# Softmax probabilities scaled ahead of their transposes, one head on VectorE and one on GpSimd

## The reference, cut to what matters

```python
def one(qblk):
    s = jnp.einsum('bqhd,bkhd->bhqk', qblk, k).astype(jnp.float32) * scale
    p = jax.nn.softmax(s, axis=-1).astype(v.dtype)
    return jnp.einsum('bhqk,bkhd->bqhd', p, v)
```

## Time and profile before

| what | value |
|---|---|
| median of 3 runs | 1138.98 us (1138.32 to 1143.58) |
| span of the profiled execution | 1138.1 us |
| TensorE busy (matmul) | 1042.1 us, 92% |
| VectorE busy | 337.7 us, 30% |
| ScalarE busy | 256.1 us, 23% |
| GpSimd busy | 113.0 us, 10% |
| DMA | 313.84 MB, mean 276 GB/s |

### The profile page before, as it was taken

One profiled execution on the slowest core, in us unless ns is written; L12 is line 12 of the kernel. 1 busy time (PEld: TensorE's weight loads), 2 busy tenths in 40 slices (PEclk: granted clock), 3 DMA queues, 4 the chain that ended last, 5 costly groups with the idle time before them and its releaser, 6 DMA issues. The chain is left out here.

```text
span 1138.1 us, 16374 instructions
## 1 busy us (share of the span) xinstructions
PE 1042.1 (92%) x6617; PEld 506.9 (45%) x6617; DVE 337.7 (30%) x838; ACT 256.1 (23%) x604; POOL 113.0 (10%) x137
## 2 busy tenths in 40 slices
PE   5899899998999999988699989999989999998967
PEld 3445456654434444333244554666444344433324
DVE  3100465412722222112330026542173222221224
ACT  2110254512211111111221014542131111111132
POOL 4120100001001111110022020000010111111000
PEclk8899999998999999999899999999989999999997
DMA  9941466614899999999994225662298999999981
GB/s 351 384 159 74 158 233 222 222 40 162 322 332 322 401 393 397 398 402 411 385 340 154 84 103 223 223 222 75 100 349 305 353 344 395 401 396 412 410 317 56
DMA packets 70291, 313.84 MB, mean 276 GB/s; under 512 B 7786, under 2 KB 10054, under 8 KB 49984
## 3 DMA queue, kind: packets, MB, share of 16 engines
q1 hardware_dynamic: 61280, 288.54, 66.3%
q0 software_dynamic: 8064, 21.01, 5.3%
q10 hardware_dynamic: 864, 3.15, 0.7%
HBM read 301.32 MB, written 18.58 MB: 281 GB/s over the span
## 5 line engine op out<-in xcount | busy, mean ns | idle before, releaser
L938 PE MATMUL psum<-arena 128*64 128x512 f32 x512 | 236.1, 608 | 18.1 <-DMA arena<-in_w_up 11.6
L941 PE MATMUL psum<-arena 128*64 128x512 f32 x512 | 236.6, 609 | 0.0
L938 PEld LDWEIGHTS psum<-arena 128*64 128x64 f32 x512 | 69.1, 140 | 164.9 <-issue 162.6
L992 PE MATMUL psum<-arena 128*64 128x512 f32 x512 | 120.5, 602 | 3.8 <-ACT arena L1399 2.1
L1775 DVE SCALAR_TENSOR_TENSOR arena<-arena,psum 64x768 f32<-64x768 f32 (+1 forms) x32 | 26.1, 814 | 273.0 <-ACT arena L1393 273.0
L1258 PE MATMUL psum<-arena 128*128 128x384 f32 x256 | 86.3, 492 | 0.0
L1393 ACT ACTIVATE arena<-psum 64x768 f32<-64x768 f32 (+1 forms) x32 | 22.3, 697 | 280.3 <-PE psum L941 280.3
L1113 PE MATMUL psum<-arena 128*128 128x384 f32 x256 | 83.5, 487 | 1.2 <-PE psum L1101 0.6
L941 PEld LDWEIGHTS psum<-arena 128*64 128x64 f32 x512 | 69.1, 140 | 0.0
L1113 PEld LDWEIGHTS psum<-arena 128*128 128x128 f32 x256 | 48.3, 190 | 36.9 <-issue 4.0
L1258 PEld LDWEIGHTS psum<-arena 128*128 128x128 f32 x256 | 47.5, 190 | 32.4 <-issue 0.7
(11 more groups left out here) (273 smaller groups left out, 1245.9 us busy)
## 6 DMA issues: line engine op xcount, KB each, us to landing
arena<-in_w_down SPq DMA_DIRECT2D x64, 1024.0 KB, 16.7
arena<-in_w_gate SPq DMA_DIRECT2D x54, 1024.0 KB, 14.5
arena<-in_w_up SPq DMA_DIRECT2D x54, 1024.0 KB, 17.0
arena<-in_w_ada SPq DMA_DIRECT2D x24, 2048.0 KB, 7.9
arena<-in_w_in SPq DMA_DIRECT2D x6, 2048.0 KB, 17.2
arena<-in_w_gate SPq DMA_DIRECT2D x20, 512.0 KB, 17.5
arena<-in_w_up SPq DMA_DIRECT2D x20, 512.0 KB, 18.5
arena<-in_w_out SPq DMA_DIRECT2D x4, 2048.0 KB, 7.9
```

The lines of the kernel that those rows point to most:

```text
L938: ins = nc.tensor.matmul(bank[b][0:MAIN, :], hg[:, k, 0:MAIN], row(wg[half], k), start=(k == 0), stop=(k == KD - 1))
L941: ins = nc.tensor.matmul(bank[b][MAIN:P, :], hg[:, k, 0:MAIN], row(wu[half], k), start=(k == 0), stop=(k == KD - 1))
L992: ins = nc.tensor.matmul(bank[6][MAIN * j:MAIN * j + MAIN, :], hidT[:, c, 0:MAIN], w[half][:, c % 2, 512 * j:512 * j + 512], start=(c == 0 ...
```

## The change

The scaling by the reciprocal sums moves from the attention output to the probabilities. After `rsum` is written, VectorE multiplies head 1's probabilities in place, and GpSimd those of head 0, in place too. TensorE waits for the product of each head before it transposes it, in place of waiting for the exponentials. The two small matmuls that spread the reciprocals go, ScalarE's copy of bank 4 is 128 columns shorter, and `outputs` becomes a copy. `reciprocals(u)` also waits until GpSimd is done with unit u-2, since it overwrites the same places of `rsum`.

```diff
+        prob_pool, prob_dve = sem("prob_pool"), sem("prob_dve")
...
         @block.gpsimd
...
                 pool.sem_inc(out_free, 1)
 
+                for u in range(UNITS):
+                    n = unit(u)[3]
+                    pool.wait_ge(rsum_ready, UNITS * l + u + 1)
+                    pool.tensor_scalar(prob[:, u % 2, 0, 0:n], prob[:, u % 2, 0, 0:n], rsum[:, 2 * (u % 2):2 * (u % 2) + 1], None,
+                                       ALU.mult).then_inc(prob_pool, 1)
...
                 def turned(u):
                     n = unit(u)[3]
-                    pe.wait_ge(exp_ready, UNITS * l + u + 1)
                     for i in (1, 0):
+                        pe.wait_ge(prob_pool if i == 0 else prob_dve, UNITS * l + u + 1)
                         if u >= 1:
                             pe.wait_ge(probT_act if i == 0 else probT_dve, UNITS * l + u)
                         for c in range(n // P):
                             ins = nc.tensor.transpose(bank[4 + i][:, P * c:P * c + P], prob[:, u % 2, i, P * c:P * c + P], ident)
-                        if i == 0:
-                            pe.wait_ge(rsum_ready, UNITS * l + u + 1)
-                            for h in range(2):
-                                r = rsum[:, 2 * (u % 2) + h:2 * (u % 2) + h + 1].to_broadcast([P, HD])
-                                ins = nc.tensor.matmul(bank[4][HD * h:HD * h + HD, n:n + P], r, ident, start=True, stop=True)
                         ins.then_inc(probT_ps, 1)
...
-                    nc.scalar.activation(probT0[:, u % 2, 0:n + P], bank[4][:, 0:n + P], ACT.Copy).then_inc(probT_act, 1)
+                    nc.scalar.activation(probT0[:, u % 2, 0:n], bank[4][:, 0:n], ACT.Copy).then_inc(probT_act, 1)
...
                     dve.wait_ge(exp_ready, UNITS * l + u + 1)
+                    if u >= 2:
+                        dve.wait_ge(prob_pool, UNITS * l + u - 1)
                     v.reciprocal(rsum[:, c:c + 2], sums[:, cs:cs + 2]).then_inc(rsum_ready, 1)
+                    dve.wait_ge(rsum_ready, UNITS * l + u + 1)
+                    n = unit(u)[3]
+                    v.tensor_scalar(prob[:, u % 2, 1, 0:n], prob[:, u % 2, 1, 0:n], rsum[:, c + 1:c + 2], None, ALU.mult).then_inc(prob_dve, 1)
...
-                    v.tensor_tensor(o, bank[6][:, 0:P], probT0[:, w % 2, n:n + P], ALU.mult).then_inc(o_ready, 1)
+                    v.tensor_copy(o, bank[6][:, 0:P]).then_inc(o_ready, 1)
```

More of the change, by code:

```diff
@@ L593, in _, with unit @@
             sp.wait_ge(stored_y, 16 * NT)
+        def unit(u):
+            kind, r = divmod(u, 12)
+            pair, t = divmod(r, 3)
+            return kind, pair, t, (P if t == 0 else TOK)
         @block.gpsimd
@@ L791, in copies_qk @@
             copy_out(eng, l, parity, IT_QK, IT_KOUT, place, width=TOK, scale=lambda i: NA_SCALE if i < 4 else 1.0)
[L793 to L796, removed]
         @block.tensor
```

## The result

The changed kernel takes 1180.37 us (median of 4 runs, 1179.10 to 1181.75) against 1139.05 us; the ratio is 1.0358, 95% interval 1.0337 to 1.0380. It is 41 us slower. The forecast was 1144 and the range ended at 1153: the sign was right, the loss was eight times the forecast one (41 us for 5).

What follows compares the result with a forecast made beforehand. TensorE was taken to bound both attentions; stalls waiting for the products, less the removed matmuls' gain, summed to +2.65 us a layer, +5.3 in all, giving 1144 us from 1138.98, with a range of 1136 to 1153.

Steps and rivals of the forecast that it cites:

- What bounds the kernel, and that a loss passes through: Both attentions: TensorE sets the time, and a microsecond won or lost there moves everything behind it in full.
- VectorE's product and the removed matmuls: Each attention step: VectorE's multiply of head 1 costs 0.44 us; dropping the spreading matmuls saves TensorE 0.27 us.
- GpSimd's product, 0.65: Each attention step: GpSimd's multiply of head 0 takes 0.65 us for 384 columns, extrapolated from earlier rows.
- The hand-off from GpSimd to TensorE, 0.20: Ahead of head 0's transposes: TensorE starts 0.20 us after GpSimd's product ends.
- The collision: First rival: both engines' multiplies contend, head 0 comes 0.28 us later in 24 steps, +7 us, 1151; chance 0.22.
- The step table: Step-by-step count of attention stalls and gains, with values at R + 1.46 where stalled: +2.65 us a layer, +5.3 together.
- step 13: Latent attention step with only 128 keys of scores as cover: values start 0.17 us later than before.
- R: The end of VectorE's reciprocals of a step's unit, which both heads' transposes wait for after the change.
- latent steps 3k+2: Latent attention steps with 384 keys of scores as cover: no stall, 0.27 us won in each.
- The clock: TensorE's granted clock, read as 1.00 in both attentions before the change; the forecast had no term for its falling.
- The third rival, a stretched chain: Around the attention: stalls and VectorE's added work delay maxima and later scores, +5 us, 1149; chance 0.10.
- V: The end on TensorE of the values matmuls of the step before, which VectorE's outputs, then reciprocals, wait for.

Runs made afterwards that it cites:

- e9: As e7, but reciprocals and products of units 3k+1 taken at the start of step 3k, ahead of VectorE's maxima; 1134.1 us, ratio 0.9973 to the kernel before.
- e5: Changed kernel with GpSimd's multiply given a second operation (adding zero) and VectorE's product of head 1 left out; 1141.5 us in one run.
- e1: Changed kernel with GpSimd's multiply given a second operation that adds zero; 1149 us, ratio 1.0100 to the kernel before.
- e6: Changed kernel with idle matmuls, results never read, put into TensorE's stalls ahead of the transposes; 1161 us, ratio 1.0215 to the kernel before.
- e4: Changed kernel without GpSimd: VectorE multiplies head 1, then head 0; 1144.3 us, ratio 1.0037 to the kernel before.
- e7: As e4, but VectorE takes the next unit's reciprocals and products one step early; 1136.0 us, ratio 0.9998 to the kernel before.
- e2: Changed kernel without VectorE's product, so head 1 is transposed undivided; 1164.1 us in one run.
- e3: Changed kernel with GpSimd's product written to an unused half of another buffer instead of in place; 1181.3 us in one run.

## Why the prediction was wrong

**What bounds the kernel, and that a loss passes through:** right. 37 of 40.7 us are in the attentions, and the rest is the output projection at the lowered clock.

**VectorE's product and the removed matmuls:** right for the product, 0.42 us for 0.44. The matmuls gave 0.22 us in each latent step and not 0.27 (e9: three steps 9.64 - 8.98 = 0.66 of 0.81). The values, which now follow the transposes directly, take 0.06 longer from start to start: 0.37 in e9 (192.95 to 193.32), 0.31 before (196.09 to the next scores at 196.40).

**GpSimd's product, 0.65:** this is the step that failed; it measured 1.47. The term was taken from rows of another form of the instruction, and I set its upper bound by VectorE's collision alone. For the two-operation form the extrapolation was right to 2% (662 ns in e5). For the form that the change uses it is 1243 ns, and 1471 beside VectorE. I had looked at shape, type and memory of the rows, and not at the number of operations.

**The hand-off from GpSimd to TensorE, 0.20:** the matmul row that I took it from names ScalarE, not GpSimd, as what ended the wait, so the row didn't carry it. It measured 0.05 to 0.06, as said above.

**The collision:** it exists. I gave it 0.28 us and a chance of 0.22, and it is 0.23 us in every product of 384 columns and 0.09 in one of 128 (448 to 540, 604 to 697), in either form. GpSimd's start-up time, which I had thought may hide most of it, hides at most 0.05 of my 0.28. The Trainium skill's rule ("GPSIMD Engine Reference", "Key points": GpSimd contends with VectorE instructions in a two-port mode) agrees with these rows. No run shows which mode VectorE was in. Alone the collision would have given about 1149 to 1150 (e1), where I had 1151.

**The step table:** right, once the term is put right. With the measured product the values of step 13 should start at R + 2.03 (1.46 + 0.82, less 0.25 for the faster hand-offs); they start at R + 2.10, and the longer transposes are the difference. Put 2.10 for 1.46 in every step that stalls, and in the latent steps 3k+2, which then stall too, and the table gives some +24 us for both attentions (an estimate from these rows); e6, with the same product at full clock, has +24.5 (181.4 - 156.9). With 662 ns (e5) my table has 9.47, 9.54 and 11.89 us for the three kinds of groups; e5 has 9.25, 9.49 and 11.40, at the faster hand-offs. The attentions of e5 and e4 are 2.8 and 3.5 us longer than before, where the sum was +5.3. In e5 head 1 isn't multiplied at all, so it is a check of the size and not of the whole change.

**The clock:** missing altogether, a term put at nothing without a reason. I had neither a term nor a rival for it. It is 16 of the 41 us (e6). The remaining 25 are the stalls at full clock. Of the 37 us in the attentions the form makes 29, stall and clock together (193.9 in the changed kernel, 164.9 in e1). Another 5 go with VectorE's product (164.9 less the 159.7 of e5); that is the collision and, since e5 leaves head 1 undivided, whatever that product costs otherwise. The last 3 are left in e5, where the forecast was 5.3. That the sign came out right is no credit to the 1144: with the collision alone the kernel would have been inside the range, and the form, which I hadn't considered, threw it out.

**The third rival, a stretched chain:** its sign is there, its cost isn't. In step 13 VectorE starts its maxima at 203.05, 0.17 us after the scores' end and not 0.05, because its product stands ahead of them, but no scores wait for that afterwards. For three latent steps of the changed kernel, at full clock, the readiness of head 0 gives: step 13 + 0.64 on my table; step 14, wanted at V + 1.73 and ready at V + 2.04, with the values 0.07 later, + 0.38; so 9.64 - 0.10 + 0.64 + 0.38 = 10.56. Measured are 10.72. By the starts, 0.05 of the 0.16 left over is in step 12 (0.22 won and not 0.27), 0.01 in step 13 and 0.11 in step 14, half of it values that take 0.81 from start to start for 0.75.

## What to carry to other kernels

Cost a new instruction from a row of the same form, down to the number of its operations, and where there is none let the range reach to what a slow form would give. A stall on a TensorE that is otherwise full can cost more than its length: here 16 of 41 us were the lowered clock behind the stalls. So give each forecast of new stalls a case in which the clock falls. And ahead of a faster operation look at where its engine's queue puts it: the same products cost 0.4% (e4), nothing (e7) or perhaps minus 0.3% (e9) by their place in VectorE's order alone.

## What the runs showed of the hardware

- GpSimd's float32 tensor_scalar with one multiply takes 604 ns for 128 columns and 1243 for 384; with a multiply and an add 448 and 662. These are the times without VectorE's product beside it (e2, e5). In both cases the scalars are pointers into SBUF.
- VectorE's 420 ns product within SBUF, started 0.06 us before GpSimd's (190.96 and 191.02), adds 226 to 228 ns to one of 384 columns, whatever its form, and isn't itself slowed (420 ns in the changed kernel, 421 in e1; head 1's product with GpSimd idle, e4, takes the same). For 128 columns it adds 92 to 93 ns.
- TensorE's granted clock fell to 0.5 behind the neighbourhood steps with 1.1 to 1.7 us of idle time ahead of head 1's transposes, and behind the last steps of the attention (0.92 and 0.56 us). In the latent steps with 0.30 and 0.56 us it stayed at 1.00. Behind the same stalls of 1.13 us it stayed at 1.00 in e3's second layer, and behind one of 2.38 us it fell in e9's first layer and not in its second. Seven idle matmuls of 128 columns in three steps kept it at 1.00 in the whole attention.
